# Dilated attention in uniform steps of 512 columns between the gate projections of an encoder layer on eight cores

## The reference

```
h = rms_norm(x, g_mix)
proj = h @ w_in            # q_A k_A v_A | q_B k_B v_B | q_M | gate logits
oa = banded attention, |i-j| <= 128, 8 heads of 64, ALiBi, a sink logit per head
for gi, (window, dil) in enumerate(((128, 1), (512, 4), (2048, 16))):   # branch B
    # stride-dil subsequences: position m*dil + r -> (r, m); 4 heads of 128 per group
    o, lse = banded_attention(gather(q), gather(k), gather(v), slopes[gi], window // (2 * dil), dil)
ob = sum over gi of softmax(lse)[gi] * o[gi]     # window is 64 on each side in every group
om = attention of the sequence into 256 memory tokens
x = x + sum_b(sigmoid(gate_b) * (o_b @ w_branch_b)) @ w_out
x = x + relu(rms_norm(x, g_mlp) @ w_up)^2 @ w_down
```

## Time and profile before

| | us |
|---|---|
| runs timed | 3158.28, 3376.23, 3462.62 (median 3376.23) |
| profiled execution | 3164.88 |
| its span on the slowest core (core 2) | 3163.8 |
| spans of the eight cores | 3140.8 to 3163.8 |
| PE busy / ACT / DVE / POOL on core 2 | 2600.8 / 1281.1 / 1328.6 / 410.3 |

### The profile page before, as it was taken

The page is one execution under the profiler, slowest core; times in us unless marked ns, Lnnn a source line. Parts: engine busy times, 40 slices in busy tenths (PEclk is TensorE's granted clock), DMA queues, the critical chain, the costliest instruction groups (busy, mean ns, idle before and its releaser), DMA issues.

```text
span 3163.8 us, 45628 instructions; the slowest of 8 cores (3140.8 to 3163.8 us)
## 1 busy us (share of the span) xinstructions
PE 2600.8 (82%) x14044; PEld 1249.5 (39%) x14044; DVE 1328.6 (42%) x2175; ACT 1281.1 (40%) x2336; POOL 410.3 (13%) x353
## 2 busy tenths in 40 slices
PE   6889988957888798654996359995779999999998
PEld 3444433323443355332553124442334444444443
DVE  5665677655664324322253246663202212322321
ACT  5666766645776665324653222222202201211210
POOL 2110000000000013221032354442000000000000
PEclk9999999988999899876998689997889999999999
DMA  6355332232223555443543857774921110110110
GB/s 151 115 136 100 78 71 79 67 89 83 73 68 100 165 157 157 121 109 113 161 151 104 206 174 234 231 234 120 191 45 58 67 49 19 67 67 1 67 54 27
DMA packets 292956, 344.73 MB, mean 109 GB/s; under 512 B 29040, under 2 KB 258160, under 8 KB 290288
## 3 DMA queue, kind: packets, MB, share of 16 engines
q1 hardware_dynamic: 260960, 299.35, 29.7%
q0 software_dynamic: 31760, 42.47, 9.4%
HBM read 257.36 MB, written 126.88 MB: 121 GB/s over the span
## 4 chain that ended last, share of the span: by engine, by line
PE 64%; DMA 10%; ACT 8%; DVE 7%; issue 7%; SPq 1%; POOL 1%; another core or an unknown queue 1%; DVEq 0%; ACTq 0%; POOLq 0%
PE p_b L1163 14%; PE p_b L1150 14%; PE p_b L549 8%; PE p_b L415 6%; PE p_b L1017 5%; PE p_b L528 4%; PE p_b L643 4%; PE p_b L1039 3%; DMA t_ksl<-sKB 3%; PE p_b L613 3%; DMA sGT<-t_gob 2%; DMA t_oT<-sOT 2%; DVE t_cpb L438 2%; PE p_b L458 2%; ACT t_lnb L460 2%
## 5 line engine op out<-in xcount | busy, mean ns | idle before, releaser
L415 PE MATMUL p_b<-t_hT,t_wt 128*128 128x512 bf16 x2112 | 502.1, 381 | 11.5 <-DVE t_hT L354 9.4
L1150 PE MATMUL p_b<-t_h2Tt,t_wup 128*128 128x512 bf16 x2048 | 445.3, 380 | 47.2 <-DMA t_h2Tt<-sH2T 47.2
L1163 PE MATMUL p_b<-t_wdn,t_upT 128*128 128x512 bf16 x2048 | 445.7, 380 | 29.2 <-DMA t_wdn<-w_down 17.0
L1154 ACT ACTIVATE t_rl<-p_b 128x512 f32<-128x512 f32 x256 | 152.8, 597 | 758.3 <-PE p_b L1150 751.4
L549 PE MATMUL p_b<-t_hT,t_wt 128*128 128x512 bf16 x1536 | 397.0, 405 | 0.0
L628 ACT ACTIVATE t_E<-p_b 128x512 bf16<-128x512 f32 (+3 forms) x492 | 228.6, 480 | 252.8 <-PE p_b L613 173.5
L1150 PEld LDWEIGHTS p_b<-t_h2Tt,t_wup 128*128 128x128 bf16 x2048 | 200.8, 98 | 290.3 <-issue 50.1
L1155 DVE TENSOR_TENSOR t_upT<-t_rl 128x512 bf16<-128x512 f32 x256 | 177.4, 693 | 319.3 <-ACT t_rl L1154 319.3
L1163 PEld LDWEIGHTS p_b<-t_wdn,t_upT 128*128 128x128 bf16 x2048 | 200.4, 98 | 274.5 <-issue 36.0
L415 PEld LDWEIGHTS p_b<-t_hT,t_wt 128*128 128x128 bf16 x2112 | 205.0, 98 | 243.6 <-issue 20.3
L1017 PE MATMUL p_b<-t_oT,t_wbr 128*128 128x512 bf16 x768 | 173.7, 386 | 72.3 <-DMA t_oT<-sOT 43.8
(11 more groups left out here) (102 smaller groups left out, 2925.4 us busy)
## 6 DMA issues: line engine op xcount, KB each, us to landing
y<-t_x SPq DMA_DIRECT2D x16, 2048.0 KB, 8.2
sGT<-t_gob SPq DMA_DIRECT2D x192, 128.0 KB, 2.4
t_gT<-sGT SPq DMA_DIRECT2D x8, 3072.0 KB, 20.5
t_wt<-w_in POOLq DMA_DIRECT2D x17, 1024.0 KB, 13.6
t_xt<-x SPq DMA_DIRECT2D x32, 512.0 KB, 7.5
t_x<-x SPq DMA_DIRECT2D x8, 2048.0 KB, 11.5
t_x<-y SPq DMA_DIRECT2D x8, 2048.0 KB, 8.2
sVB<-t_vst SPq DMA_DIRECT2D x24, 512.0 KB, 3.1
```

What stands on the lines that cost most here:

```text
L415: i = h.matmul(a[:, :], lhsT=w[:, kc, u["wcol"]:u["wcol"] + 128], rhs=rhs[:, kc, t * TT:(t + 1) * TT], start=(kc == 0), stop=(kc == 7))
L1150: ins = h.matmul(U[:, :], lhsT=wup[:, kc, c * 128:(c + 1) * 128], rhs=hT_[:, kc, :], start=(kc == 0), stop=(kc == 7))
L1163: ins = h.matmul(A[:, :], lhsT=upT[:, c, s * 128:(s + 1) * 128], rhs=wdn[:, c, half * 512:(half + 1) * 512], start=(c == 0), stop=(c == 31))
```

## The change

Branch B. Every item has now 512 score columns. A tile of groups 0 and 1 loads a window of 384 keys that starts 64 keys ahead of its 256 queries, in three chunks of 128 which serve 128, 256 and 128 queries; an item is one head of it (`tile_items`: 4 items a tile, each with 3 score matmuls and 6 products). At a sequence's two ends the missing 64 keys are filled with other keys and masked to zero by a factor from `params` (`P_EDGE`); in 10 of the 32 tiles this costs three further small transfers, one into `ksl` and two into `vsl`. Group 2 takes two subsequences at a time (`pair_items`): three items, one for each subsequence's own 128 keys and one for both halves of 64 queries that look into the other chunk. `load_pair` issues five transfers, two of them into `qtb` and two into `vsl`. A half has 8 pairs (24 items) and 16 tiles (64 items); both halves, 176 items, run as one list. The order of the groups is now 2, 1, 0, so that group 2 copies (D on ACT, N on DVE) and groups 1 and 0 add. The exponential writes into the buffer that the mask multiply then works on in place.

Gates. 192 units over 168 steps, 1.14 a step. The store of a unit is issued two units later, from 6 buffers instead of 2. The last 64 units run by token tile, and behind the gates of token tile t the weights of the merge are loaded into the part of `hT` that tile t-1 has left; `hT` is eight tensors now.

Divisions. `b_final` of a quarter is cut into three posts (Ln, Exp, multiplies with the store) behind the tile of group 0 that completes the quarter, and the result is written into `Nacc`.

```
+            if k < 4 and c == 3 and t == NTT - 1:
...
-            go, bgo = gob[i], b_gob[i]
+            gi_ = gob_n[0] % len(gob)
+            gob_n[0] += 1
+            go, bgo = gob[gi_], b_gob[gi_]
...
-            cx.dma(sp, bgo, GT[j][:, t * TT:(t + 1) * TT], go[:], reads=[bgo], writes=[b_GT[j][t]])
+            g_late.append(lambda: cx.dma(sp, bgo, GT[j][:, t * TT:(t + 1) * TT], go[:], reads=[bgo],
+                                         writes=[b_GT[j][t]]))
+            while len(g_late) > 2:
+                g_late.pop(0)()
...
+        g_units = [(lambda k=k, c=c, t=t: f_gate(k, c, t)) for k in range(4) for c in range(4) for t in range(NTT)]
+        for t in range(NTT):
+            for k in (4, 5):
+                for c in range(4):
+                    g_units.append(lambda k=k, c=c, t=t: f_gate(k, c, t))
+                    if k == 4 and c == 2 and 1 <= t <= 5:
+                        g_units[-1] = lambda t=t, f=g_units[-1]: (f(), p3_weights(t - 1))
...
+            lst, k, src, nm = (wbr, i, w_br_d, "wbr") if i < 3 else (wout, i - 3, w_out_d, "wout")
+            lst[k] = place("%s%d" % (nm, k), [128, 4, D], BF16, 2 + 8 * i)
+            cx.dma(pool, lst[k][1], lst[k][0][:], src[512 * k:512 * (k + 1), :].rearrange("(kc p) n -> p kc n", p=128),
+                   writes=[lst[k][1]])
...
+                        if it.get("inplace"):
+                            E_, bE = P_, bP
+                        else:
...
+                            else:
+                                cx.op(me, lambda h: h.tensor_tensor(out=view(P_), in0=view(E_), in1=m_ap, op=ALU.mult),
+                                      reads=[bE] + it["mask_bufs"], writes=[bP])
                 pump.step()
                 if i >= LAG:
                     it = items[i - LAG]
@@ -644,8 +681,8 @@
                                            stop=it["stop"], skip_group_check=True)
                         return ins
...
-                        pending.append((i + 1, it["post"], it["grp_id"], it["bank"]))
+                    for k_, f in enumerate(it.get("post", ())):
+                        pending.append((i + 1 + k_, f, it["grp_id"], it["bank"]))
...
-        Nacc, b_nacc = place("Nacc", [128, 4, 2048], F32, 82, 4)
-        Dacc, b_dacc = place("Dacc", [128, 4, 2048], F32, 114, 4)
...
+        Nacc, b_nacc = place("Nacc", [128, 4, 2048], F32, 82, 16)
+        Dacc, b_dacc = place("Dacc", [128, 4, 2048], F32, 114, 16)
...
+        tgb, b_tgb = zip(*[place("tgb%d" % i, [128, TT], F32, 194 + 2 * i) for i in range(2)])
+        gob, b_gob = zip(*[place("gob%d" % i, [128, TT], BF16, 198 + i) for i in range(6)])
...
+        def b_final(S2, q4):
+            lo, hi = q4 * 512, (q4 + 1) * 512
+            bn, bd = acc_bufs(b_nacc, range(4), lo, hi), acc_bufs(b_dacc, range(4), lo, hi)
+            def f1():
+                cx.op(act, lambda h: h.activation(out=Dacc[:, :, lo:hi], in_=Dacc[:, :, lo:hi], func=AF.Ln),
+                      reads=bd, writes=bd)
...
+            def f2():
+                cx.op(act, lambda h: h.activation(out=Dacc[:, :, lo:hi], in_=Dacc[:, :, lo:hi], func=AF.Exp, scale=-1.0),
...
+            def f3():
+                out = Nacc[:, :, lo:hi].bitcast(BF16)[:, :, 0:512]
+                for hh in range(4):
+                    e = dve if hh % 2 == 0 else pool
+                    b1, b2 = bn[hh:hh + 1], bd[hh:hh + 1]
+                    cx.op(e, lambda h: h.tensor_tensor(out=out[:, hh, :], in0=Nacc[:, hh, lo:hi], in1=Dacc[:, hh, lo:hi],
+                                                       op=ALU.mult), reads=b1 + b2, writes=b1)
+                t0 = S2 * 2048 + lo
+                cx.dma(sp, bn[0], OT[4:8, :, t0:t0 + 512].rearrange("c p t -> p c t"), out, reads=bn,
+                       writes=[b_OT[1][t0 // 256], b_OT[1][t0 // 256 + 1]])
+            return f1, f2, f3
...
+                if first:
+                    cx.op(act, lambda h: h.activation(out=da, in_=dv_, func=AF.Copy), reads=[b_bank[kd]], writes=bd_)
+                    cx.op(dve, lambda h: h.tensor_copy(out=na, in_=nv_), reads=[b_bank[kn]], writes=bn_)
...
+            k_lo, k_hi = p0 - 64, p0 + 320
+            lo, hi = max(0, k_lo), min(Ls, k_hi)
+            bk, bv = b_ksl[i2], b_vsl[i2]
+            kparts = [(lo, hi, lo - k_lo)]
+            vparts = []
+            if k_lo < 0:
+                kparts.append((0, 64, 0))
+                vparts += [(0, 64, 0, 0), (0, 64, 64, 0)]
+            if k_hi > Ls:
+                kparts.append((Ls - 64, Ls, 320))
+                vparts += [(Ls - 64, Ls, 0, 2), (Ls - 64, Ls, 64, 2)]
+            for k0, k1, c0 in kparts:
+                cx.dma(sp, bk, ksl[i2][:, :, c0:c0 + k1 - k0], KQ(KB, k0, k1), reads=rd(b_KB, k0, k1), writes=[bk])
+            rows = lambda k0, k1: VB[g, k0 * d + r:(k1 - 1) * d + r + 1:d, :]
+            c_lo, c_hi = (1 if k_lo < 0 else 0), (2 if k_hi > Ls else 3)
+            k0, k1 = k_lo + 128 * c_lo, k_lo + 128 * c_hi
+            cx.dma(sp, bv, vsl[i2][:, c_lo:c_hi, :], rows(k0, k1).rearrange("(kc a) c -> a kc c", a=128),
+                   reads=[b_VB[g][t] for t in keys_of(d, k0, k1)], writes=[bv])
+            for k0, k1, a0, kc in vparts:
+                cx.dma(sp, bv, vsl[i2][a0:a0 + 64, kc, :], rows(k0, k1),
+                       reads=[b_VB[g][t] for t in keys_of(d, k0, k1)], writes=[bv])
...
+        def load_pair(ti, r, S2):
+            i2 = ti % RB
+            for rr in range(2):
+                c0 = (r + rr) * 256 + S2 * 128
+                cx.dma(sp, b_qtb[i2], qtb[i2][:, :, 128 * rr:128 * rr + 128],
+                       QB[8:12, :, c0:c0 + 128].rearrange("c p t -> p c t"), reads=[b_QB[8 + c][t] for c in range(4)
+                                                                                   for t in range(NTT)],
+                       writes=[b_qtb[i2]])
+            cx.dma(sp, b_ksl[i2], ksl[i2][:], KB[8:12, :, r * 256:r * 256 + 512].rearrange("c p t -> p c t"),
+                   reads=[b_KB[8 + c][t] for c in range(4) for t in range(NTT)], writes=[b_ksl[i2]])
+            for kc in range(2):
+                src = VB[2, 2048 * kc:2048 * (kc + 1), :].rearrange("(a rr) c -> a rr c", rr=16)[:, r:r + 2, :]
...
+            parts = [(1, 0, 256, 128), (0, 0, 128, 0), (2, 128, 128, 384)]
...
+            for h0 in (0, 2):
...
+                for hb in range(2):
+                    hh = h0 + hb
+                    j = 4 * g + hh
+                    s_list, pvl, starts = [], [], []
+                    for kc, q0, n, c0 in parts:
+                        s_list.append((ksl[i2][:, hh, 128 * kc:128 * kc + 128], qtb[i2][:, hh, q0:q0 + n], c0, 1))
+                        for kk, st in ((kn, vsl[i2][:, kc, hh * 128:hh * 128 + 128]), (kd, ones128[:])):
+                            pvl.append((bank[kk][:, 256 * hb + q0:256 * hb + q0 + n], st, c0, n))
+                            starts.append(hb == 0 and kc == 1)
...
+                    items.append(dict(
+                        nq=512, s_list=s_list, kq_bufs=[b_ksl[i2], b_qtb[i2]], scale=sc_b, shift=-SHIFT_B,
+                        mask=mask, mask_bufs=[b_wbt], inplace=True, pv=pvl, starts=starts, stop=hb == 1,
+                        v_bufs=[b_vsl[i2], b_ones], pool_share=not edge, out_bufs=[b_bank[kn], b_bank[kd]],
+                        grp_id=gi, bank=gi % 2))
...
+                items[-1]["post"] = (b_post(first, d, h0, 2, 256, nat0, kn, kd, gi),)
+            if last and (p0 // 256) % 2 == 1:
+                items[-1]["post"] += b_final(S2, (p0 - S2 * half) // 512)
...
+            for rr, (gi, kn, kd) in enumerate(groups):
+                s_list, pvl, starts = [], [], []
+                for hh in range(4):
+                    s_list.append((K(hh, rr, S2), qtb[i2][:, hh, 128 * rr:128 * rr + 128], 128 * hh, 1))
+                    for kk, st in ((kn, V(hh, rr, S2)), (kd, ones128[:])):
+                        pvl.append((bank[kk][:, 128 * hh:128 * hh + 128], st, 128 * hh, 128))
+                        starts.append(hh == 0)
+                items.append(dict(common, s_list=s_list, mask=[(lambda T: T[:, :], WOt[:, :, :].rearrange("p b q -> p (b q)"))],
+                                  pv=pvl, starts=starts, stop=False, out_bufs=[b_bank[kn], b_bank[kd]], grp_id=gi,
+                                  bank=gi % 2))
...
+            for rr, (gi, kn, kd) in enumerate(groups):
+                for hh in range(4):
+                    c0 = 256 * rr + 64 * hh
+                    s_list.append((K(hh, rr, 1 - S2), qtb[i2][:, hh, 128 * rr + q0:128 * rr + q0 + 64], c0, 1))
+                    for kk, st in ((kn, V(hh, rr, 1 - S2)), (kd, ones128[:])):
+                        pvl.append((bank[kk][:, 128 * hh + q0:128 * hh + q0 + 64], st, c0, 64))
+            m_ap = WSt[:, S2, :, :].rearrange("p b q -> p (b q)").unsqueeze(1).to_broadcast([128, 2, 256])
+            items.append(dict(common, s_list=s_list, mask=[(blocks(512, 2), m_ap)], pv=pvl, starts=[False] * len(pvl),
```

(32 more changed lines are left out.)

316 lines of the change are left out of this document (147 added, 169 removed).

## The result

The changed kernel is faster: the ratio of its times to those of the kernel before is 0.965, 95% interval 0.961 to 0.970. The profiled execution took 3045.8 us (3164.9 before); the forecast was 3023 for 3165, a ratio of 0.955. So the sign, the class and the rough size came out as forecast, the gain 119 us instead of 142.

A forecast was written before the change was run, and what follows sets the result against it. PE bounds groups 0 and 1; exposed load latency behind gate stores bounds group 2. Terms 341 + 173 + 20 + 16 + 15 + 61 = 626 us for 768, 142 less: 3023 from 3164.9, range 2955 to 3120.

The forecast's parts named there:

- Sequence ends: Ten tiles with chained k and v loads hold SP about 14 us each; 2 us a tile, 20 us together.
- Divisions: Ln and Exp in ACT's queue cost PE 0 to 4 us a quarter; taken as 2 x 8, 16 us.
- Its own sign for groups 0 and 1: The prediction is wrong if groups 0 and 1 take more than 364 us; forecast 341 us.
- Group 2: SP's chained loads and stores set the pace: 16 pairs at 10.8 us, 173 us, bounds 126 and 200 us.
- the half boundary: The new half's first copies wait for the last division's store out of `Nacc`: 8 us (0 to 12).
- the sign of being wrong named for group 2: The prediction is wrong if PE waits in group 2 for DVE or ACT.
- DVE's waits down from 109 us: DVE's waits for `sGT` gate stores fall from 109 us, with what is left at sequence ends.
- Start of the merge: Last division 10 us, `gT` and `oT` 25, merge steps 25: 61 us (50 to 75), where it took 100.
- Loss in groups 0 and 1: 5% added to 325 us of PE work in groups 0 and 1, giving 341; bounds 0 and 12%.
- single places: Branch start 3 us, half boundary 8, weights of gates 20 to 23 4: 15 us together.
- PE's pace in group 2: Rival: load latencies overlap better, 7.9 us a pair, 47 us less, 2976 us; chance 0.13.
- Losses stay: Rival: groups 0 and 1 keep their 12% (+23), sequence ends and divisions cost double (+36): 3082 us; chance 0.17.

The follow-up runs named there:

- parts_ends: The changed kernel with only the extra loads of the ten tiles at sequences' ends freed from one another, pairs still chained: 3018.7 us, ratio 0.954.
- parts_no_div: parts_all without the Ln and Exp of the eight divisions on ACT, so the output is undivided: 2942.8 us, ratio 0.934.
- weights_last: The changed kernel with the merge's weights all loaded after the last gate instead of under the gates: 3058.6 us, ratio 0.970.
- before_late: The kernel before with gate stores issued two units later, out of four buffers instead of two: 3031.9 us, ratio 0.961.
- parts_pairs: The changed kernel with only load_pair's q and v parts freed from one another, sequence-end loads still chained: 3011.7 us, ratio 0.953.
- parts_all: The changed kernel with each part of a q, k or v buffer given its own dependency, so no loads are chained: 2982.7 us, ratio 0.942.

## Why the prediction was right and wrong

**The steps that failed** are three terms of F, each too small while the order of events was as told. Sequence ends were put at 20 us and measured 41 (parts_ends). Divisions were put at 16 and measured 33 ahead of the last product (parts_no_div). And the merge's weights under the last gates had no term at all in the branch: the prediction's reason was that the DMA engines are 0.54 to 0.57 busy there, and weights_last shows that they cost 23 to 28 us of it. The first and the third overlap, since the blocks lengthen the holds at sequence ends. Its own sign for groups 0 and 1, more than 364 us, came too: they took 410.9, of which 74 are ends and divisions, and the 337 left are what it had forecast for the rest (341).

**The balance.** F falls from 616.2 to 481.4 us by the late stores and their buffers alone (532 - 50.4). From there the change's other parts go up again: 481.4, plus 3 for columns, plus 33 for divisions, plus 77 for chained loads is 594, which is what the changed kernel has. What they win lies outside F: the stretch between the halves (50.4) and 37.6 us of head (100.7 to 63.1). That is 113 lost against 88 won: 632.5 us from first score to first wa product in before_late, 657.2 in the changed kernel. All but the 3 us are each from a pair of traces; that they close to a microsecond is partly luck, since traces of one kernel differ by some. The 77 us hold a part of what the merge's weights cost; no run has both edits.

**Group 2: mechanism right, size short.** 16 pairs at 10.8 us were forecast; they took 10.9 each in the first half and 12.0 in the second, 183 us for 173. It lies inside the bounds. What the chained loads cost in it was put at 47 us over PE's pace. That parts_pairs gave 48 us of F back is luck: only 33 of them came in the pairs, which then still took 151 us and not 126. SP without a gap in the first half's pairs was right. In the second half one wait of 12.5 us is the half boundary, put at 8 with bounds of 0 and 12: DVE's first copy waits 8.3 us of it for the last division's store. So the sign of being wrong named for group 2, PE waiting there for DVE, came with 23 us, beside 32 for k.

**Sequence ends: undersized.** The step took SP as held for 14 us, and without a weight block beside it that is right: 9.9 to 13.8 us. With one it is 17.7 to 20.2, at five of the ten. Over all ten it is 15.3 us, so the hold is off by little, and what it costs PE by more: parts_ends gave 41 us of F back, 4 us a tile where 2 were forecast, inside the bounds of 0 and 5. That step also read "DVE's waits down from 109 us"; they rose to 117.5. Before, they came from two buffers (four leave 16.7 us of them, four and late stores 6.6); now they come from stores that stand behind chained loads (the split leaves 2.0). The list of waits gives both the same name.

**Divisions: undersized by half.** 16 us forecast, 33 measured, of which 18 are table loads that I had taken as "inside the same allowance". The condition that I had written down, "It is wrong if ACT's switches show up as PE waits of over 4 us", was nearly the right alarm: the longest of PE's waits for a tanh is 3.9 us, and one division's cost is spread over several small waits on masks and tanh.

**Start of the merge: right.** 61 us forecast, 63.1 measured. The chain that ended last has, in its own order, the last Ln and Exp (1.92 each), two multiplications of together 3.44 and this transfer, the 22.9 us of the earlier trace rows again:

```profile
1708.02 23.03 DMA t_oT<-sOT
```

**Loss in groups 0 and 1.** 5% and 15 us for single places, 31 in all; the kernel without chained loads, Ln and Exp has F = 484.1 for 451 of PE's need, 33. As a sum that allowance was right, though these 33 us also hold what group 2 loses there.

**The sum.** 565 us forecast for F, 594.1 measured: +10 chained loads, +17 divisions, +2 the rest. From first score to first wa product it is 657.2 instead of 626 us; 10 us came back behind the merge's start: 5 in the rest of the merge and 6 in the MLP (1008.6 us on core 2 before, 1002.6 on core 7 now), whose code the change leaves alone. The cores of one execution of the kernel before lie up to 23 us apart, so these 10 us may be no gain of the change.

**The rivals.** PE's pace in group 2 (2976) did not come: where second loads don't wait, in parts_pairs, the time is 3011.7 us and a pair takes 9.4 us, not 7.9. That parts_all comes to 2982.7 is a likeness of numbers, since it frees the sequence ends too. The 2.3 and 2.6 us worked out there for single loads are not what this trace has either: the second of two chained q loads of 128 KB was issued 2.6 to 4.8 us after the first. Losses stay (3082) had two right terms: ends and divisions did cost double (74 us for 36). Its third, 12% in groups 0 and 1, did not come, and the truth lies between it and the forecast. No rival said what mattered most, that one part of the change alone has all its gain: I had read in the earlier trace rows that the store ahead of the loads waits for the gate, and yet never wrote the sum for that part by itself. Written, it would have been the 156 us of the earlier trace rows less the 46.1 between the halves, 110 us, of which before_late gave 89.

## What to carry to other kernels

A queue that holds both loads and stores has a wait in it wherever a store is issued as soon as its producer is: price that order first and alone, since two more buffers and a store two units later were worth 4% here, and the rest of the change nothing more until its loads were parted. In the changed kernel, whose loaders stand three steps or more ahead, the delay by itself was worth nothing. When a tile is filled by several loads, give each its own dependency: chained on one queue they cost 77 us that no engine's busy time shows. A wait for a free buffer says only that the store is late; look at the queue ahead of the store before adding buffers. And a load that is moved under other work is not free because the DMA engines have idle time: 10 MB of weights under the gates cost 23 to 28 us there to save 34 behind them.

## What the hardware showed that I had not expected

Copies of 512 elements out of PSUM to addresses with a stride of 16, from the list of lines of the changed kernel; on ACT it is 1.04 us where the plain copy into `rD` takes 0.59, on DVE 1.02:

```profile
L908 ACT ACTIVATE t_Dacc<-p_b 128x512 f32<-128x512 f32 x32 | 33.3, 1040 | 2.6 <-POOL t_Nacc L891 2.6
L909 DVE COPY t_Nacc<-p_b 128x512 f32<-128x512 f32 x32 | 32.8, 1023 | 9.0 <-DMA sOT<-t_Nacc 8.3 <-DVE t_gob L567 0.7
```

Group 2's clock went from 0.77 to 0.92 in before_late with no more work in it, only less standing still. A wait on PE cost its own length and slower matmuls behind it: in the changed kernel the gate behind the 16.0 us wait at the branch's start shows 3.31 us, the next one 1.89. And a reciprocal on DVE takes 3.3 us for 512 elements, where ACT's two passes take 3.8 us for 2,048.
